# A two-block transformer on one core: cross attention fed tile by tile from an output scaled in PSUM, and the last feed-forward's weight sums made at four places

## The chip, the cores and the metric

The program runs on one core of one Trainium2 chip. The metric is the device time of one execution in microseconds (us), of which the median over three runs is given. The core has a matrix engine (TensorE, PE), a vector engine (VectorE, DVE), a scalar engine (ScalarE, ACT), a general engine (GpSimd, POOL), and SyncE (SP), which only issues transfers here. Each engine runs its own instructions in order, and they meet at semaphores. Transfers between HBM and the on-chip memory SBUF are made by 16 DMA engines, which all queues share; TensorE writes its products to PSUM, which VectorE and ScalarE read.

## The reference, cut to what matters

Two transformer blocks of width 1024 on 512 tokens (the second has 16 more). What the change touches:

```python
def first_block(...):
    h = h + hybrid_mixer(rmsnorm(h, norm_mix_g[l]), ...)           # ends with y_all @ w_out
    h = h + memory_cross_attention(rmsnorm(h, norm_xa_g[l]), mem, norm_mem_g[l],
                                   w_xq[l], w_xk[l], w_xv[l], w_xo[l])
    h = h + sqrelu_mlp(rmsnorm(h, norm_ff_g[l]), w_ff1[l], w_ff2[l])
    ...
def memory_cross_attention(hn, mem, ...):
    q = (hn @ w_q).reshape(b, s, XA_HEADS, XA_HEAD_DIM)            # 4 heads of 128
    logits = jnp.einsum("bshd,bmhd->bhsm", q, k) * (1.0 / math.sqrt(XA_HEAD_DIM))
    p = jax.nn.softmax(logits, axis=-1)
    ...
def gla_mixer(h, w_in, w_a1, w_a2, b_a, g_out, w_out):
    ...
    return (o * jax.nn.silu(r)) @ w_out                            # o normalised per head
def swiglu(h, w_in, w_out):
    gate, up = jnp.split(h @ w_in, 2, axis=-1)
    return (jax.nn.silu(gate) * up) @ w_out
```

## The kernel before, in words

**Products.** Activations lie feature-major: `h` holds 8 tiles of 128 features by 528 tokens. Every float32 operand is split into a high and a low part of a faster type, and a product is three matmuls (hi by hi, low by hi, hi by low). Weights come in units of 1 MB (128 x 2048): SP loads a unit to `w_raw` (two buffers), ScalarE writes `w_hi` (L491), VectorE, in some layers GpSimd, writes `w_lo = w_raw - w_hi` (L498), each two buffers deep. `sp_unit` loads unit u as soon as the low part of unit u-2 is made. A tile's sum lies in PSUM in `lin[slot]`, slot 0 or 1 with two banks each; whoever takes it out raises `lin_taken0` or `lin_taken1`, and TensorE waits for that before it reuses the slot (`deep=True` uses both banks of a slot, and waits for one tile less).

**Norms.** A layer's RMS norm is applied after its product: as each tile of `h` is finished, ScalarE writes the high part of the next operand (L794) and the tile's square (L912), VectorE the low part (L917, `dve_operand`), and GpSimd adds up the squares (L932, `pool_squares`). When all eight squares are added, TensorE sums over the partitions (L952, `pe_squares`), ScalarE takes the root, VectorE the reciprocal (L1001, `dve_root`), and the product is scaled by `scale_d`.

**From the mixer to cross attention.** `WB` is the second half of the mixer's output product (8 tiles, two units). `dve_mix_output` takes each tile out: it multiplies by `scale_d` into `tmp` (L737) and adds that to `h` (L740), then writes the low part of the tile before. `pe_cross` then makes the four query tiles (`query(t)`, L1807, 24 matmuls each, two tiles a unit), with the eight operand tiles waited for one by one in `query(0)`; between `query(0)` and `query(1)` stand the norm's sums. `logits(0)` (L1817) needs query 0 scaled (L1924), and so the reciprocal. The low parts of the next weight units are VectorE's: one in the middle of the mix output, one ahead of `dve_root`.

**Quads.** In the feed-forward layers most weight units are "quad" units: a product of 2 x 2 blocks is made with 7 block products in place of 8, and needs sums of weight blocks. These sums are made in HBM by transfers that GpSimd issues, in rounds for each group of layers ("ff1", "up0", "up1"): `pool_quad_base` copies the units to `weight_sums` (L385), `pool_quad_pairs` adds one block to another (L391, L393), `pool_quad_triples` (L399) and `pool_quad_fours` (L407) go on from there, each round after the one before has landed. The up1 group (parts a, b, c with 5, 7 and 5 units, for the last feed-forward, from 1667 us on) has its rounds issued from the queue of GpSimd between its other work, in program order. SP loads for a quad unit three blocks (L419), one sum (L421), and, when the last quad's `w_sum` buffer is free, the other three sums (L425, 768 KB).

**Gated linear attention (GLA).** `GR` is its gate product (8 tiles of 528 tokens, in 4 units); GpSimd makes the low parts of its weights (`dve_splits(pool, GR, nc.gpsimd)`). `dve_gates` takes each tile out (L1010), ScalarE applies silu (L2415), GpSimd multiplies it with the attention's output (`pool_gates`, L2464), VectorE scales it (L2487), ScalarE writes the high part (L2432) and VectorE the low part (L2492). The next product, `GOUT`, begins with `pe_first_pair` (L608): its two first tiles, with these eight operands waited for.

## Time and profile before

| | |
|---|---|
| median of 3 runs | 2020.7 us (2017.12 to 2021.94) |
| profiled execution, its own time | 2011.54 us |
| span of its trace | 2009.7 us |
| mean granted clock of TensorE | 0.991 of full speed |
| busy: PE, DVE, ACT, POOL | 97%, 63%, 42%, 15% of the span |

The profile is of one execution. Times in its views are microseconds from the start of the span; 1.8 us of the execution's time lie outside the span. "Busy" of the matrix engine includes pipelined matmuls whose ends are modelled, so its waits are read from single rows rather than from its share.

### The profile page before, as it was taken

How to read it: one execution, taken by the hardware profiler on the slowest of the kernel's cores; microseconds unless marked ns; L12 is line 12 of the kernel's file. 1: busy time of each engine (PE TensorE's matmuls, PEld its weight loads, DVE VectorE, ACT ScalarE, POOL GpSimd, SP SyncE). 2: the span in 40 equal slices, each digit the busy share in tenths (PEclk: the TensorE clock that was granted, in tenths of full speed). 3: DMA queues.
4: the chain of work that ended last, by engine and by line, in shares of the span. 5: the costliest groups of instructions: out<-in, count | busy, mean ns of one | idle time of the engine just before them, and what ended most of it. 6: DMA issues, size and time to landing. Idle time of an engine off the chain costs nothing.

```text
span 2009.7 us, 29776 instructions
## 1 busy us (share of the span) xinstructions
PE 1939.4 (97%) x12259; PEld 1709.5 (85%) x12259; DVE 1269.4 (63%) x1770; ACT 838.5 (42%) x1140; POOL 305.2 (15%) x249
## 2 busy tenths in 40 slices
PE   7999998999999899999999999999998899999998
PEld 6788866788898888999999999999885578889896
DVE  6668767666574664121658577476798658668475
ACT  4448744433142344223444143244534445234243
POOL 2122241200110141011420000002144110000002
PEclk9999999999999999998999999999998999999999
DMA  9854131499999758810165343343221023344251
GB/s 332 218 120 146 64 89 65 178 352 248 221 246 337 275 128 199 171 50 35 65 165 191 121 148 137 116 152 117 83 84 54 22 100 132 125 157 159 100 186 66
DMA packets 68480, 299.14 MB, mean 149 GB/s; under 512 B 6505, under 2 KB 6633, under 8 KB 48386
## 3 DMA queue, kind: packets, MB, share of 16 engines
q1 hardware_dynamic: 38064, 201.15, 27.9%
q0 software_dynamic: 30128, 96.08, 20.2%
q8 instruction: 95, 1.56, 0.3%
q14 instruction: 31, 0.25, 0.0%
q10 hardware_dynamic: 162, 0.10, 0.0%
HBM read 295.19 MB, written 94.96 MB: 194 GB/s over the span
## 4 chain that ended last, share of the span: by engine, by line
PE 55%; issue 27%; DVE 9%; ACT 3%; DMA 3%; POOL 2%; SPq 0%; POOLq 0%; DVEq 0%; ACTq 0%
PE lin L584 32%; PE lin L2015 7%; PE aux L2015 5%; DMA w_sum<-weight_sums 2%; DVE scores L2781 1%; DVE best L2776 1%; PE lin L1807 1%; PE aux L1605 1%; PE aux L2911 1%; POOL squares L932 1%; ACT w_hi L491 1%; DMA w_raw<-in_weights 1%; PE lin L1560 1%; DVE w_lo L498 1%; PE lin L2881 1%
## 5 line engine op out<-in xcount | busy, mean ns | idle before, releaser
L584 PE MATMUL lin<-x_hi,w_hi 128*128 128x512 f32 (+1 forms) x1128 | 397.2, 352 | 9.4 <-issue 2.9
L584 PE MATMUL lin<-x_hi,w_lo 128*128 128x512 f32 (+1 forms) x1128 | 396.0, 351 | 0.0
L584 PE MATMUL lin<-x_lo,w_hi 128*128 128x512 f32 (+1 forms) x1128 | 395.5, 351 | 0.0
L498 DVE TENSOR_TENSOR w_lo<-w_raw,w_hi 128x2048 fp32r<-128x2048 f32 (+1 forms) x102 | 231.0, 2265 | 144.7 <-ACT w_hi L491 144.3
L491 ACT ACTIVATE w_hi<-w_raw 128x2048 fp32r<-128x2048 f32 (+1 forms) x112 | 210.3, 1878 | 207.7 <-PE lin L584 193.1
L584 PEld LDWEIGHTS lin<-x_hi,w_hi 128*128 128x128 f32 x1128 | 211.9, 188 | 43.1 <-issue 6.7
L584 PE MATMUL lin<-v_hi,w_hi 128*128 128x264 f32 (+1 forms) x704 | 236.7, 336 | 6.1 <-DVE tmp L2567 3.5
L584 PEld LDWEIGHTS lin<-x_lo,w_hi 128*128 128x128 f32 x1128 | 212.0, 188 | 29.9 <-issue 0.2
L584 PEld LDWEIGHTS lin<-x_hi,w_lo 128*128 128x128 f32 x1128 | 212.0, 188 | 29.7
L584 PE MATMUL lin<-v_hi,w_lo 128*128 128x264 f32 (+1 forms) x704 | 233.5, 332 | 0.0
L584 PE MATMUL lin<-v_lo,w_hi 128*128 128x264 f32 (+1 forms) x704 | 233.1, 331 | 0.0
L932 POOL TENSOR_TENSOR squares<-squares,tmp 128x512 f32<-128x512 f32 (+2 forms) x64 | 87.3, 1364 | 617.8 <-ACT tmp L912 615.2
L584 PEld LDWEIGHTS lin<-v_hi,w_hi 128*128 128x128 f32 x704 | 133.9, 190 | 21.7 <-issue 7.8
L584 PEld LDWEIGHTS lin<-v_lo,w_hi 128*128 128x128 f32 x704 | 133.9, 190 | 13.3 <-issue 0.5
L584 PEld LDWEIGHTS lin<-v_hi,w_lo 128*128 128x128 f32 x704 | 133.8, 190 | 12.6
L456 DVE TENSOR_TENSOR w_lo<-w_raw,w_hi 128x512 fp32r<-128x512 f32 x129 | 110.4, 865 | 39.6 <-ACT w_hi L433 20.1
L433 ACT ACTIVATE w_hi<-w_raw 128x512 fp32r<-128x512 f32 x43 | 27.1, 631 | 196.5 <-PE lin L2015 109.2
L2015 PE MATMUL aux<-v_hi,w_hi 128*128 128x256 f32 (+1 forms) x344 | 97.0, 282 | 0.4 <-DVE tmp L2041 0.4
L2015 PE MATMUL aux<-v_hi,w_lo 128*128 128x256 f32 (+1 forms) x344 | 97.3, 283 | 0.0
L2015 PE MATMUL lin<-vt_lo,w_hi 128*128 128x256 f32 (+1 forms) x344 | 97.1, 282 | 0.0
L2015 PE MATMUL lin<-vt_hi,w_hi 128*128 128x256 f32 (+1 forms) x344 | 97.0, 282 | 0.0
L2015 PE MATMUL aux<-v_lo,w_hi 128*128 128x256 f32 (+1 forms) x344 | 96.8, 281 | 0.0
(481 smaller groups left out, 4437.1 us busy)
## 6 DMA issues: line engine op xcount, KB each, us to landing
w_raw<-in_weights SPq DMA_DIRECT2D x112, 1024.0 KB, 4.8
w_raw<-in_weights SPq DMA_DIRECT2D x43, 768.0 KB, 6.0
w_sum<-weight_sums SPq DMA_DIRECT2D x43, 768.0 KB, 4.7
weight_sums<-in_weights POOLq DMA_DIRECT2D x4, 5120.0 KB, 48.7
weight_sums<-in_weights POOLq DMA_DIRECT2D x2, 7168.0 KB, 56.2
w_raw<-weight_sums SPq DMA_DIRECT2D x43, 256.0 KB, 6.3
weight_sums<-in_weights POOLq DMA_DIRECT2D x8, 1280.0 KB, 13.9
weight_sums<-weight_sums POOLq DMA_DIRECT2D x8, 1280.0 KB, 12.5
```

The lines of the kernel that those rows point to most:

```text
L433: nc.scalar.activation(w_block(w_hi, unit, 1, 2), w_block(w_raw, unit, 1, 2), ACT.Copy)\
L456: nc.vector.tensor_tensor(w_block(w_lo, unit, a, b), w_block(w_raw, unit, a, b), w_block(w_hi, unit, a, b).bitcast(F32), ALU.subtract)\
L491: nc.scalar.activation(w_hi[:, s, 0:n], w_raw[:, s, 0:n], ACT.Copy).then_inc(sem("w_hi_ready"), 1)
L498: does.tensor_tensor(w_lo[:, s, 0:n], w_raw[:, s, 0:n], w_hi[:, s, 0:n].bitcast(F32), ALU.subtract).then_inc(sem("w_lo_ready"), 1)
L584: last = nc.tensor.matmul(o, a, b, start=(k % (L.kc // k_banks) == 0 and p == 0), stop=((k + 1) % (L.kc // k_banks) == 0 and p == 2))
L932: nc.gpsimd.tensor_tensor(acc, acc, tmp[:, s, 0:N.n], ALU.add).then_inc(sem("square_added"), 1)
L1560: mm = nc.tensor.matmul(lin[1][64 * (hd % 2):64 * (hd % 2) + 64, 1, P * j:S1], v_tok[:, j, 64 * hd:64 * hd + 64], w_att[:, SB_AT[j]:SB_AT[ ...
L1605: mm = nc.tensor.matmul(o, wp[:, k, t % 4 * P:t % 4 * P + P], xp_[:, k, 0:S1], start=(k == 0 and r == 0), stop=(k == 3 and r == 2))
L1807: mm = nc.tensor.matmul(lin[slot][:, 0, :], wp[:, k, m * P:m * P + P], xp_[:, k, 0:S1], start=(k == 0 and p == 0), stop=(k == KD - 1 and p ...
L2015: mm = nc.tensor.matmul(bank[:, b, 0:hf], wp, xp_, start=(k == 0 and p == 0), stop=(k == 3 and p == 2))
L2776: ins = nc.vector.max(best[:, n - 1, :], scores_of(n))
L2781: ins = nc.vector.match_replace(scores_of(n), best[:, n - 1, :], scores_of(n), TAKEN)
```

## The change

- **The mix output.** The product is scaled in place, in PSUM, and then added to `h` from there; `lin_taken` is raised by the add and `h_added` by a no-operation behind it. The split of the next weight unit stands two tiles earlier on ScalarE and on VectorE.
- **Cross attention.** The first two query tiles are made together (`first_queries`): operands 0 to 3 for the one and then the other, then operand after operand for both. The norm's sums come behind both, and then 14 matmuls whose product nobody reads. The low part of the second query unit moves from VectorE to GpSimd.
- **GLA's end.** `pe_first_pair` takes operands 0 to 3 for its first tile, 0 to 3 for its second, and 4 to 7 for both, one by one. The last gate tile is taken out and passed through silu after operand 3 and ahead of operands 4 to 7.
- **The up1 sums.** GpSimd issues the copies of part b where all three stood, those of a and c only behind the squares of the next norm, and the three transfers of the triples one by one between GR's four weight units.

```diff
@@ dve_mix_output
-                ht, out_t = h_tile(t, S1), tmp[:, 2 + t % 2, 0:S1]
+                ht, out_t = h_tile(t, S1), lin[slot][:, t // 2 % 2, 0:S1]
                 dve.wait_ge(sem("lin_done"), n + 1)
-                nc.vector.tensor_tensor(out_t, lin[slot][:, t // 2 % 2, 0:S1], scale_d[:, 0:S1], ALU.mult)\
-                    .then_inc(sem(f"lin_taken{slot}"), 1)
+                link(dve, nc.vector.tensor_tensor(out_t, out_t, scale_d[:, 0:S1], ALU.mult))
+                nc.vector.tensor_tensor(ht, ht, out_t, ALU.add).then_inc(sem(f"lin_taken{slot}"), 1)
                 dve.wait_ge(sem(f"lin_taken{slot}"), before + 1)
-                nc.vector.tensor_tensor(ht, ht, out_t, ALU.add).then_inc(sem("h_added"), 1)
-                dve.wait_ge(sem("h_added"), base + t + 1)
+                nc.vector.engine_nop().then_inc(sem("h_added"), 1)
                 if t:
                     dve_operand(dve, l_xa, t - 1)
-                if t == 5:
+                if t == 3:
                     next_lo(dve, WB, 1, 0)
@@ pe_cross (a step is the three matmuls of L1807)
+                pe.wait_ge(sem("w_lo_ready"), w_unit + 1)
+                for m in range(2):
+                    slot, before, _ = XQ.tile(0, m, 0)
+                    pe.wait_ge(sem(f"lin_taken{slot}"), before - 1)
+                    for k in range(4):
+                        if m == 0:
+                            l_xa.wait_operand(pe, k)
+                        step(m, k)
+                for k in range(4, KD):
+                    l_xa.wait_operand(pe, k)
+                    for m in range(2):
+                        mm = step(m, k)
+                        if k == KD - 1:
+                            mm.then_inc(sem("lin_done"), 1)
@@
-            query(0)
+            first_queries()
             pe_squares(pe, l_xa)
-            query(1)
+            for _ in range(14):
+                nc.tensor.matmul(lins[:, 1, 0:S1], v_hi[:, 0, 0:P], v_hi[:, 0, 0:S1], start=True, stop=True)
             logits(0)
@@ dve_cross
-            next_lo(dve, XQ, 0, 0)
             dve_root(dve, l_xa)
             taken(0)
             taken(1)
             maxima(0)
+            dve.wait_ge(sem("w_lo_ready"), XQ.unit0 + 2)
             next_lo(dve, XQ, 1, 0)
@@ pe_first_pair
-                for k in range(L.kc - 1):
+                for k in range(L.kc // 2):
                     if m == 0:
                         ready(k)
                     step(m, k)
-            ready(L.kc - 1)
-            for m in range(2):
-                step(m, L.kc - 1).then_inc(sem("lin_done"), 1)
+            for k in range(L.kc // 2, L.kc):
+                ready(k)
+                for m in range(2):
+                    mm = step(m, k)
...
@@ dve_gates, t == KD - 1
-                    for k in range(KD - 1):
+                    for k in range(4):
                         scaled(k)
                         if k:
                             lo(k - 1)
-                    lo(KD - 2)
...
-            scaled(KD - 1)
+            for k in range(4, KD):
+                scaled(k)
+                lo(k - 1)
             lo(KD - 1)
@@ the queue of GpSimd
             pool_squares(pool, l_xa, l_ssd.idx + 1)
+            next_lo(pool, XQ, 0, 0, nc.gpsimd)
             pool_squares(pool, l_ff, l_ff.idx)
...
-            pool_quad_base(pool, "up1", *"abc")
+            pool_quad_base(pool, "up1", "b")
             pool_squares(pool, l_mix0, l_mix0.idx)
+            pool_quad_base(pool, "up1", *"ac")
             pool_quad_pairs(pool, "up1")
-            pool_quad_triples(pool, "up1")
             next_splits_after(pool, GR)
-            dve_splits(pool, GR, nc.gpsimd)
+            for u in range(GR.units):
+                next_lo(pool, GR, u % 2, u // 2, nc.gpsimd)
+                if u < len(SUM_RUNS["up1"]):
+                    pool_quad_triple(pool, "up1", u)
             pool_gates(pool)
```

The order of instructions on VectorE in the mix output, its first tiles, before (L737 scales, L740 adds, L917 is the low part of the tile before):

```order
L737 TENSOR_TENSOR tmp<-lin,scale_d 128x512
L740 TENSOR_TENSOR h<-h,tmp 128x512
L917 SCALAR_TENSOR_TENSOR v_lo<-h,col,v_hi 128x512
L498 TENSOR_TENSOR w_lo<-w_raw,w_hi 128x2048
L737 TENSOR_TENSOR tmp<-lin,scale_d 128x512
L740 TENSOR_TENSOR h<-h,tmp 128x512
```

That piece is from tiles 5 and 6. The corresponding piece of the change, from tiles 3 and 4 (the lines have moved by 6 to 9):

```order
L746 TENSOR_TENSOR lin<-lin,scale_d 128x512
L747 TENSOR_TENSOR h<-h,lin 128x512
L749 ISA
L925 SCALAR_TENSOR_TENSOR v_lo<-h,col,v_hi 128x512
L504 TENSOR_TENSOR w_lo<-w_raw,w_hi 128x2048
L746 TENSOR_TENSOR lin<-lin,scale_d 128x512
L747 TENSOR_TENSOR h<-h,lin 128x512
```

The scaled product no longer passes through `tmp`, each tile has one no-operation more, and the weight's low part stands two tiles earlier. On TensorE the place behind the last operand now reads (L960 the norm's sum, L1889 the 14 idle matmuls, L1849 the first logits):

```order
L1812 MATMUL lin<-v_hi,w_hi 128x512
L1812 MATMUL lin<-v_lo,w_hi 128x512
L1812 MATMUL lin<-v_hi,w_lo 128x512
L960 MATMUL aux<-squares,cst 128x512
L1889 MATMUL lin<-v_hi 128x512 x14
L1849 MATMUL aux<-k_t,xq_t 128x256 x4
```

Before, the 24 matmuls of query 1 stood between the norm's sum and the logits; they now stand ahead of the sum. On GpSimd, between the copies of up1 and GLA's gates, before:

```order
L385 DMA weight_sums<-in_weights 128x5x2048
L385 DMA weight_sums<-in_weights 128x7x2048
L385 DMA weight_sums<-in_weights 128x5x2048
L925 MEMSET squares 128x1056
...
L399 DMA weight_sums<-weight_sums 128x5x512
L399 DMA weight_sums<-weight_sums 128x7x512
L399 DMA weight_sums<-weight_sums 128x5x512
...
L498 TENSOR_TENSOR w_lo<-w_raw,w_hi 128x2048
```

and with the change:

```order
L385 DMA weight_sums<-in_weights 128x7x2048
L933 MEMSET squares 128x1056
...
L385 DMA weight_sums<-in_weights 128x5x2048 x2
L391 DMA weight_sums<-in_weights 128x5x512
...
L504 TENSOR_TENSOR w_lo<-w_raw,w_hi 128x2048
L405 DMA weight_sums<-weight_sums 128x5x512
L504 TENSOR_TENSOR w_lo<-w_raw,w_hi 128x2048
L405 DMA weight_sums<-weight_sums 128x7x512
```

Two of the three copies move behind the eight rounds of squares (in a loop, whose rows are left out), and each triple stands behind a weight unit's low part.

## Rows read from the trace of the kernel before

**Rows 1.** The page: the span, and the chain that ended last.

```profile
span 2009.7 us, 29776 instructions
PE 55%; issue 27%; DVE 9%; ACT 3%; DMA 3%; POOL 2%; SPq 0%; POOLq 0%; DVEq 0%; ACTq 0%
```

**Rows 2.** Waits of PE: for whom, us in total, times, longest.

```profile
PE lin L1807 <- DVE w_lo L498: 6.3, 1, 6.3
...
PE lin L584 <- DVE h L689: 2.9, 2, 1.6
...
PE lin L608 <- DVE x_lo L2492: 1.0, 3, 0.4
```

**Rows 3.** Windows over ff1c's and ff1d's quads: stretch, length, PE busy (matmuls), others.

```profile
564.43:594.23 29.80, 29.80 (x254) 29.80 (x253) 24.08 (x34) 13.28 (x19) 3.17 (x2) 1.00 1.05 244
650.00:686.18 36.18, 30.27 (x252) 29.75 (x252) 23.89 (x34) 13.21 (x18) 0.00 (x0) 1.00 0.96 356
```

**Rows 4.** The three-sums load: the page's median, then 622 to 645 us.

```profile
w_sum<-weight_sums SPq DMA_DIRECT2D x43, 768.0 KB, 4.7
w_sum<-weight_sums SPq DMA_DIRECT2D x1, 768.0 KB, 20.4
```

**Rows 5.** Timeline of POOL: start, us, instruction, idle before it.

```profile
449.46 1.47 POOL L391 DMA_DIRECT2D weight_sums<-in_weights  x1 [66.01 <-DMA weight_sums<-in_weights]
...
602.81 2.42 POOL L385 DMA_DIRECT2D weight_sums<-in_weights  x2
...
736.70 1.48 POOL L391 DMA_DIRECT2D weight_sums<-in_weights  x1
...
798.04 1.44 POOL L393 DMA_DIRECT2D weight_sums<-in_weights  x1 [10.88 <-issue]
...
871.84 4.55 POOL L498 TENSOR_TENSOR w_lo<-w_raw,w_hi 128x2048 fp32r<-128x2048 f32 x1 [36.66 <-ACT w_hi L491]
```

**Rows 6.** Plain weight loads (L416), all 110: from issue to landing.

```profile
DMA to landing us min/median/max: 4.6/4.8/17.1
```

**Rows 7.** Timelines of SP and ACT: one load and the split that needs it.

```profile
738.93 0.33 SPq L416 DMA_DIRECT2D w_raw<-in_weights  x1
...
760.22 1.92 ACT L491 ACTIVATE w_hi<-w_raw 128x2048 fp32r<-128x2048 f32 x1 [11.35 <-PE lin L584]
```

**Rows 8.** Timelines of DVE and POOL in the mix output.

```profile
297.11 0.68 DVE L737 TENSOR_TENSOR tmp<-lin,scale_d 128x512 f32<-128x512 f32 x1
297.83 1.78 DVE L740 TENSOR_TENSOR h<-h,tmp 128x512 f32<-128x512 f32 x1
299.65 0.75 DVE L917 SCALAR_TENSOR_TENSOR v_lo<-h,col,v_hi 128x512 fp32r<-128x512 f32 x1
...
297.76 1.30 POOL L932 TENSOR_TENSOR squares<-squares,tmp 128x512 f32<-128x512 f32 x1 [1.91 <-ACT tmp L912]
```

**Rows 9.** Timelines of DVE and POOL where the add reads PSUM.

```profile
360.17 0.68 DVE L689 TENSOR_TENSOR h<-h,lin 128x512 f32<-128x512 f32 x1
...
360.07 1.34 POOL L932 TENSOR_TENSOR squares<-squares,tmp 128x512 f32<-128x512 f32 x1 [44.87 <-ACT tmp L912]
```

**Rows 10.** The chain in cross attention: start, us, what.

```profile
306.47 7.21 PE lin L1807 x24
313.68 0.86 PE aux L952 x2
314.53 5.59 PE lin L1807 x24
```

**Rows 11.** Timelines of DVE and ACT around the norm's root.

```profile
305.69 0.68 DVE L737 TENSOR_TENSOR tmp<-lin,scale_d 128x512 f32<-128x512 f32 x1
...
315.96 3.35 DVE L1001 RECIPROCAL scale_d<-scale_d 128x512 f32<-128x512 f32 x1
...
314.57 0.69 ACT L982 ACTIVATE scale_d<-aux,eps_t 128x512 f32<-128x512 f32 x1 [0.86 <-PE aux L952]
```

**Rows 12.** A window behind the long wait; third from the end is the granted clock.

```profile
306.40:309.20 2.80, 2.73 (x7) 2.18 (x8) 2.73 (x4) 1.24 (x2) 0.90 (x2) 0.50 0.82 281
```

More of the change, by code:

```diff
@@ L400, in pool_quad_triples, with pool_quad_triple @@
                     .then_inc(sem("sum_s2"), 16)
+        def pool_quad_triple(pool, group, n):
+            pool.wait_ge(sem("sum_pair"), 2 * sums_made(group))
+            run = SUM_RUNS[group][n]
+            pool.dma_start(quad_rows(run, w_sums, 1, 2), quad_rows(run, w_sums, 3, 4), accum_op=ALU.add)\
+                .then_inc(sem("sum_s2"), 16)
         def pool_quad_fours(pool, group):
@@ L619, in pe_first_pair @@
                     step(m, k)
-            ready(L.kc - 1)
-            for m in range(2):
-                step(m, L.kc - 1).then_inc(sem("lin_done"), 1)
+            for k in range(L.kc // 2, L.kc):
+                ready(k)
+                for m in range(2):
+                    mm = step(m, k)
+                    if k == L.kc - 1:
+                        mm.then_inc(sem("lin_done"), 1)
         def act_evacuate(act, L, tile, after=None):
@@ L724, in act_mix_output @@
                 act_operand(act, l_xa, t, t % 2)
-                if t == 4:
+                if t == 2:
                     next_hi(act, WB, 1, 0)
@@ L1795, in pe_cross, with first_queries, step @@
             w_unit = XQ.unit0
+            def first_queries():
+                w = [x[:, w_unit % 2, :].rearrange("p (k n) -> p k n", k=KD) for x in (w_hi, w_lo)]
+                def step(m, k):
+                    slot = XQ.tile(0, m, 0)[0]
+                    for p, (wp, xp_) in enumerate(((w[0], v_hi), (w[0], v_lo), (w[1], v_hi))):
+                        mm = nc.tensor.matmul(lin[slot][:, 0, :], wp[:, k, m * P:m * P + P], xp_[:, k, 0:S1],
+                                              start=(k == 0 and p == 0), stop=(k == KD - 1 and p == 2))
+                    return mm
+                pe.wait_ge(sem("w_lo_ready"), w_unit + 1)
[11 more added lines that the diff above has]
+                        if k == KD - 1:
+                            mm.then_inc(sem("lin_done"), 1)
             def query(t):
@@ L2448, in act_gates @@
                             scale(e)
+                    silu(t)
+                    if t == 7:
                         for k in range(4, 7):
                             hi(k)
-                    silu(t)
                     if t == 5:
```

2 lines of the change are left out of this document (removed).

## The prediction

> **What bounds the kernel now.** I read the page first: the chain that ended last is TensorE's for more than half the span, and another quarter is "issue", time with nothing shown to wait for, much of it stretches in which TensorE runs and the chain was followed along another engine's queue [rows 1]. So time is won where TensorE stands still. The view of waits, for TensorE, gives the places: 6.3 us in one piece ahead of cross attention's first query, and in GLA's last product three short waits for operands and one for `h` [rows 2] (the 2.9 us are two waits; the one in GLA, 1.6 us, is the longest). One loss is not named there as a wait for data; two windows show it. ff1c's three quads take 29.8 us with 254 matmuls. ff1d's, the same work, take 36.2 us, with TensorE busy for 30.3 [rows 3]. The view of transfers says why: the load of the three block sums, 4.7 us in the median, took 20.4 us there [rows 4], and the timeline of GpSimd shows what it shared the DMA engines with, the copies of up1, issued from 602.81 us on [rows 5].
>
> **Part 1, the sums of up1.** The up1 copies are 17 units. up0's, of the same size, kept GpSimd waiting 66.0 us until 449.46 us [rows 5]. With the change only b's 7 units are copied behind 602.8 us: 66 x 7/17 = 27 us, more while weight loads run beside them, so they land between 630 and 640 us. The first quad of ff1d needs its sums at about 641 us, the two others later, by when nothing runs beside their loads. I take the whole difference of the two windows, 36.2 - 29.8 = **-6.4 us** [rows 3]. Bounds: nothing, if b alone fills the stretch; 6.4, since ff1c is the same work with no wait.
>
> The copies of a and c move behind 736.7 us. Ten units at the same rate are 39 us, with loads beside them up to 51, so the pairs begin at some 788 us at the latest instead of 736.70. Their issue took from 736.70 to 799.5 us [rows 5], 63 us, so GpSimd is through at about 851 us; it next has to be there at 871.84 us, for the low part of GR's weights, which ScalarE releases [rows 5]: 21 us to spare, **cost nothing**. Queued behind those transfers on GpSimd are GR's four low parts, whose readers are TensorE and SP's next load, and then GLA's gates. The triples are issued behind a low part each, 1.5 us, in time that GpSimd idles: nothing, too. The plain loads meet the copies instead. A load issued at 738.93 us is needed by the split at 760.22, which waited for TensorE and not for it [rows 7]: 21.3 us to spare, and the slowest of all 110 plain loads, those beside the copies of now among them, took 17.1 [rows 6]. Nothing again, with a small reserve.
>
> The Trainium skill (DMA: Bandwidth & Descriptors, "Issuing engines are not separate DMA queues") says that transfers issued from any engine run on the same 16 DMA engines and interleave. That speaks against this part: the copies are as large at 736 us as at 602. By it alone the 6.4 us would be paid elsewhere and the sum would be -5.0; the rows above say that the loads there have room which ff1d's have not. What hangs on it is the first rival.
>
> **Part 2, the mix output and cross attention.** The add of SBUF to SBUF took 1.78 us beside GpSimd's squares, whose instruction ran 1.30 us, and it ended half a microsecond behind it. The low part took 0.75, the scaling out of PSUM 0.68 [rows 8]. An add with the product in PSUM took 0.68 us inside a GpSimd instruction of the same kind [rows 9]. So with the change the add falls to 0.68, though the low part, which still reads two SBUF operands, will sometimes meet GpSimd and lose some tenths. A tile took 0.68 + 1.78 + 0.75 = 3.2 us, and takes 0.68 + 0.68 + 0.75 and about 0.2 for the no-operation and such a meeting, 2.3 to 2.4. Tile 4 began at 297.11 [rows 8]; it loses about one microsecond of earlier holds and gains the 2.3 us weight split that now stands ahead of it: 298.5. Four tiles more at 2.4 bring the last operand at about 308.5.
>
> TensorE's wait of 6.3 us is put down to the weight split, but it ended at 306.47, 0.1 us behind the scaling of tile 6 (305.69 + 0.68) [rows 10, 11]: it was the slot. That is now needed for tile 4 only, whose add ends at 299.9, before TensorE is done with the product ahead at 306.47 - 6.3 = 300.2. It begins there, with operands 0 to 3, and has 24 matmuls of two tiles before it needs operand 4. At 0.233 us (5.59 / 24 [rows 10]) the 48 matmuls end at 311.4; operand 7 is wanted at about 310, so 308.5 is early enough, and the squares are added by 310. There is no slow clock either: seven matmuls behind the 6.3 us wait ran at a granted clock of 0.50, the lower of the two levels, 1.2 GHz [rows 12], 0.4 us each, some 1.2 us lost.
>
> From the norm's sum it goes on in series: 0.86 (sum), 0.69 (root), 3.35 (reciprocal), 0.69 (query 0 scaled) and 0.3 between them, 5.9 us [rows 10, 11]. Before, the reciprocal began 0.7 us behind the root's end, VectorE being at a weight split; that split is now GpSimd's (4.55 us for one of this size [rows 5]), from 310.1 to 314.8, wanted at about 319 for query 2. The logits begin at 311.4 + 5.9 = 317.3 instead of 314.53 + 5.59 = 320.1: **-2.8 us**, less than the 6.3, because query 1 no longer covers the root. The 14 idle matmuls take 3.3 of these 5.9 us and cost nothing. What follows the logits keeps its distance. Bounds: -0.5, if VectorE is held as before (then only the reciprocal's 0.7 us goes), and -4, if the clock and the operands leave no seam.
>
> The Trainium skill (SBUF — State Buffer, "Who interferes with whom") has it that a VectorE instruction with two SBUF inputs, and not one with a single one, contends with a GpSimd instruction that reads SBUF. The adds agree (1.78 against 0.68), no row of before shows a long reciprocal beside GpSimd. By the rule it stays at 3.35; were it held until 314.8, the term would be -1.2.
>
> **Part 3, GLA's end.** The last gate tile's silu, gate and scaling stood behind seven operands, and the last operand, the weight split and the first addition to `h` behind them. With the tile taken out after operand 3, its own silu, gate and scaling run beside operands 4 to 6. I put the last operand about 2 us earlier (an estimate: some three instructions of 0.7 us, as those of [rows 8], leave the series), and ScalarE and VectorE come to the next split and the first `h` by as much. TensorE's waits there, 1.0 us for operands and 1.6 for `h` [rows 2], shrink to about 0.5: **-2.1 us**. Bounds 0 and -2.6.
>
> **The sum.** -6.4 - 2.8 - 2.1 = -11.3 us against the profiled execution's 2011.54: 2000.2. The median of the runs is 9.2 us above that execution, so the same difference from it gives **2009.4 us**. No change and this measurement differ by up to 0.3%, 6 us.
>
> **Rivals.**
> - *The copies are paid for in GLA.* If loads beside them take over 21.3 us, each split waits. For: transfers were at the limit in ff1d [rows 4]. Against: 17.1 at most [rows 6]. At 23 us for three units the price is about 5: 2014.5. Chance 0.13.
> - *b alone still disturbs ff1d.* It is the largest part; if it lands at 655 us, one of the loads is still slow and half of the 6.4 stays: 2012.6. Chance 0.12.
> - *Cross attention gives nothing.* The low parts take the adds' place in being held, or the last operand comes late: -0.5 in place of -2.8, 2011.7. Against: only one of three VectorE instructions a tile is left that can be held. Chance 0.1.
> - *Slower: GpSimd comes late to GR.* Copies and pairs in series must be issued by 871.84 us; from there each microsecond later costs one. It decides past 871.84 + 11.3 = 883 us, when the 114 us of both take 28% longer than I reckon; at 895 the kernel takes 2033. Chance 0.05.
>
> **How the numbers follow.** All three parts as reckoned, 0.6, own range 2006 to 2013, 2009.4 at its middle. The second and third rival lie inside or at its edge, the first within 0.3%. Range 2004 to 2016: below, the bounds of parts 2 and 3 (-1.7) and the spread of the medians before; above, the first rival. Faster by over 0.3% (below 2014.6) holds for the likeliest case, the second and third rivals and a part of the first: 0.82. Within 0.3%: 0.12. Slower: 0.06.
>
> **What the changed profile would show.** ff1d's quads at about 30 us and the three-sums loads near 5 us in the last two quads; the adds at 0.69 us, no wait of TensorE ahead of cross attention, the logits 5.9 us behind the norm's sum; GpSimd idle ahead of GR's first low part, released by ScalarE; no split in 740 to 860 us released by a DMA; no wait for `h` at GLA's end above 0.6 us. A weight load above 21 us, or GR's low part released by a transfer, would make the prediction wrong.

## The result, and the profile after

Five runs of the changed kernel took 2002.86 us in the median (2000.47 to 2009.09), five of before beside them 2019.62 (2017.12 to 2021.94): ratio 0.9922, 95% interval 0.9903 to 0.9941. The kernel is faster, and by more than forecast: 2009.4 was predicted, with a range from 2004 to 2016. The profiled execution took 2002.86 us. Against the profiled execution of before (2011.54) that is -8.7 us, against the medians -16.8; half of this study is about that disagreement. A median of five runs carries scatter of its own: 13 runs of the changed kernel, taken together further down, have a mean of 2004.6 us, inside the forecast range.

The page of the changed kernel, its span and its chain; TensorE has a larger share of the chain:

```profile
span 2001.0 us, 29796 instructions
PE 62%; issue 23%; DVE 8%; ACT 3%; POOL 3%; DMA 1%; SPq 0%; POOLq 0%; DVEq 0%; ACTq 0%
```

Windows over ff1c's and ff1d's quads, as [rows 3] (stretch, length, then busy time of PE, PEld, DVE, ACT and POOL with instructions, granted clock, DMA share, GB/s):

```profile
561.42:591.22 29.80, 29.80 (x253) 29.76 (x253) 24.20 (x35) 13.34 (x19) 3.17 (x2) 1.00 1.03 240
646.88:676.44 29.56, 29.56 (x252) 29.56 (x251) 24.09 (x34) 13.11 (x18) 0.00 (x0) 1.00 0.37 134
```

ff1d's quads took 29.6 us in place of 36.2, and the DMA engines were busy for 0.37 of the stretch in place of 0.96. Of ff1d's three three-sums loads the first (issued at 618.77 us) still took 20.2 us, ahead of the first quad and harmless; the others took 4.6 and 4.4. The copy of b, issued at 599.36 us, took 40.7 us where 27 and "more" were reckoned; it was there at 640 us, 7 us before the first quad.

GpSimd's timeline, as [rows 5]:

```profile
726.96 1.75 POOL L385 DMA_DIRECT2D weight_sums<-in_weights  x2
767.97 1.47 POOL L391 DMA_DIRECT2D weight_sums<-in_weights  x1 [39.26 <-DMA weight_sums<-in_weights]
...
825.08 1.44 POOL L393 DMA_DIRECT2D weight_sums<-in_weights  x1 [9.41 <-issue]
865.33 4.56 POOL L504 TENSOR_TENSOR w_lo<-w_raw,w_hi 128x2048 fp32r<-128x2048 f32 x1 [38.80 <-ACT w_hi L497]
```

The copies of a and c were there after 41 us (39 to 51 were reckoned), the last pair was issued at 825, and GpSimd then stood still for 38.8 us until ScalarE released GR's low part. The plain loads issued beside the copies (727 to 870 us) took 4.7 to 11.5 us; nothing waited for one.

The chain in cross attention, as [rows 10]:

```profile
300.14 11.18 PE lin L1812 x48
311.32 0.87 PE aux L960 x2
312.19 0.02 issue
312.21 0.70 ACT scale_d L990
312.91 0.02 issue
312.94 3.36 DVE scale_d L1009
316.30 0.02 issue
316.32 0.70 DVE xq_t L1957
317.02 0.04 issue
317.07 1.99 PE aux L1849 x8
```

The logits begin at 317.07 where 317.3 was forecast, 3.05 us before those of the kernel before. The reciprocal took 3.36 us though GpSimd's weight split ran beside it until 314.2, so the prediction's -1.2 for that case did not come. VectorE and GpSimd in the mix output, as [rows 8]: the adds take 0.69 us, and where something is held it is the low part, which still reads two SBUF operands:

```profile
301.11 0.69 DVE L747 TENSOR_TENSOR h<-h,lin 128x512 f32<-128x512 f32 x1
301.83 1.10 DVE L925 SCALAR_TENSOR_TENSOR v_lo<-h,col,v_hi 128x512 fp32r<-128x512 f32 x1
...
301.08 1.30 POOL L940 TENSOR_TENSOR squares<-squares,tmp 128x512 f32<-128x512 f32 x1 [1.59 <-ACT tmp L920]
```

The end of GLA. First two windows of before: its last product, and what TensorE then waits for the first addition to `h`; then the same two of the changed kernel.

```profile
970.25:983.50 13.25, 12.27 (x97) 11.63 (x95) 8.45 (x12) 6.71 (x11) 1.79 (x2) 1.00 0.00 0
983.50:985.37 1.87, 0.28 (x3) 0.10 (x2) 1.73 (x2) 0.05 (x1) 0.00 (x0) 1.00 0.00 0
```

```profile
965.18:976.78 11.60, 11.60 (x97) 11.48 (x95) 10.27 (x12) 5.85 (x9) 2.20 (x2) 1.00 0.00 1
976.78:977.24 0.46, 0.28 (x4) 0.10 (x2) 0.31 (x1) 0.06 (x1) 0.00 (x0) 1.00 0.00 0
```

15.1 us became 12.1. So the three places together gained 3.05 + 6.6 + 3.05 = 12.7 us, yet the end came only 8.7 sooner. Windows over the whole stretch between ff1d's quads and GLA's last product, of before and of the changed kernel, show where the rest went:

```profile
686.18:970.25 284.07, 281.86 (x1962) 258.19 (x1963) 105.59 (x128) 98.98 (x137) 66.12 (x36) 0.98 0.46 114
676.44:965.18 288.74, 286.53 (x1964) 262.84 (x1962) 105.00 (x127) 99.81 (x139) 67.17 (x38) 0.96 0.56 148
```

The same work took 4.7 us longer at a lower granted clock: TensorE spent 13.7 us of it at the low level (0.50) in the one execution and 23.9 in the other, which at half speed is 5.1 us lost. Nothing but GpSimd's own transfers waited for a DMA there, though the copies of a and c now run beside this work. Kernels below speak against them as the cause, with one execution each: from the norm's sum ahead of GLA to the next layer's, e_sums, with the copies there, took 290.90 us at a clock of 0.96, and m_psum, without them, 291.01 at 0.97, c_before 294.10 at 0.96.

Of the waits of TensorE in the changed kernel one is new:

```profile
PE lin L2916 <- ACT v_all L2842: 5.2, 1, 5.2
```

It lies in the attention stage, which the change does not touch; before, this wait was 1.1 us. VectorE's timeline there, first of before, then of the changed kernel, then GpSimd's of the changed kernel:

```profile
1476.39 3.44 DVE L1088 RECIPROCAL rstd<-rstd 128x528 f32<-128x528 f32 x1
1479.87 1.45 DVE L1097 SCALAR_TENSOR_TENSOR c_t<-c_t,col,rstd 128x528 f32<-128x528 f32 x2
```

```profile
1468.36 3.44 DVE L1096 RECIPROCAL rstd<-rstd 128x528 f32<-128x528 f32 x1
1471.83 5.90 DVE L1105 SCALAR_TENSOR_TENSOR c_t<-c_t,col,rstd 128x528 f32<-128x528 f32 x2
```

```profile
1472.53 4.63 POOL L504 TENSOR_TENSOR w_lo<-w_raw,w_hi 128x2048 fp32r<-128x2048 f32 x1 [6.57 <-ACT w_hi L497]
```

The two scalings of `c_t` read two SBUF operands each. In before GpSimd's weight split began at 1480.58, with the second scaling already begun, and was itself held (5.24 us for 4.63). In the changed kernel the second scaling was held through the whole split: the pair took 5.90 us against 1.45. VectorE's top-k, the longest work of the stage, stands behind it. The Trainium skill (SBUF — State Buffer, "Who interferes with whom") says that a VectorE instruction's second SBUF input comes through a port that it shares with GpSimd, and that the shared pair is "an exclusive lock". The rows agree that the one held waits for the other's instruction to end. They don't tell who gets the lock: VectorE's recorded start was 0.03 us ahead of GpSimd's in before, where it was spared, and 0.01 us ahead in the changed kernel, where it was held.

Yet this is not where the 4.0 us are missing. The attention stage from TensorE's last product ahead of it to its own last product, of before, of the changed kernel, and of a kernel tested below (f_after), where `c_t` is spared on purpose:

```profile
1516.60:1597.04 80.44, 65.87 (x267) 38.59 (x268) 60.61 (x135) 40.40 (x108) 29.18 (x35) 0.92 0.07 21
1508.55:1588.40 79.85, 62.50 (x267) 37.81 (x268) 64.12 (x148) 41.41 (x112) 29.15 (x35) 0.94 0.07 21
1508.99:1584.29 75.30, 61.07 (x268) 36.59 (x268) 60.48 (x135) 40.40 (x108) 29.18 (x35) 0.98 0.08 22
```

With `c_t` held the stage took 0.6 us less than before with it spared. The changed kernel lost 4.1 us at the start of the stage; before lost 4.7 us more than it further on. Part of that is low clock, 13.6 us at the low level against 10.2, which is worth 1.7 us at most; where the rest went is not shown. So in this pair the shortfall is the clock in the GLA stretch, and not `c_t`, though sparing `c_t` can pay, as f_after shows.

### The profile page after: what moved, and what is told of

It is laid out like the page before. It is cut to its first block, busy times and chain, and to the rows that moved or that the text cites. A ratio compares the mean times of both kernels' runs of the same rounds, so it can differ in the third digit from the quotient of the medians.

```text
span 2001.0 us, 29796 instructions
## 1 busy us (share of the span) xinstructions
PE 1940.7 (97%) x12273; PEld 1714.6 (86%) x12273; DVE 1267.6 (63%) x1769; ACT 838.4 (42%) x1140; POOL 309.1 (15%) x250
## 3 DMA queue, kind: packets, MB, share of 16 engines
q0 software_dynamic: 30128, 96.08, 20.2%
## 4 chain that ended last, share of the span: by engine, by line
PE 62%; issue 23%; DVE 8%; ACT 3%; POOL 3%; DMA 1%; SPq 0%; POOLq 0%; DVEq 0%; ACTq 0%
PE lin L590 36%; PE lin L2048 7%; PE aux L2048 5%; DVE scores L2816 1%; DVE best L2811 1%; PE aux L1613 1%; POOL squares L940 1%; PE aux L2946 1%; PE lin L1568 1%; PE lin L2916 1%; PE aux L2384 1%; ACT w_hi L497 1%; PE aux L2398 1%; DVE scores L2794 1%; DMA w_raw<-in_weights 1%
## 5 line engine op out<-in xcount | busy, mean ns | idle before, releaser
L590 PEld LDWEIGHTS lin<-x_hi,w_lo 128*128 128x128 f32 x1128 | 212.0, 188 | 29.6
L590 PEld LDWEIGHTS lin<-v_lo,w_hi 128*128 128x128 f32 x704 | 134.9, 192 | 13.3 <-issue 0.5
L462 DVE TENSOR_TENSOR w_lo<-w_raw,w_hi 128x512 fp32r<-128x512 f32 x129 | 110.4, 866 | 38.8 <-ACT w_hi L439 20.1
## 6 DMA issues: line engine op xcount, KB each, us to landing
weight_sums<-in_weights POOLq DMA_DIRECT2D x8, 1280.0 KB, 13.3
```

Of the source, the lines that this page charges most:

```text
L462: nc.vector.tensor_tensor(w_block(w_lo, unit, a, b), w_block(w_raw, unit, a, b), w_block(w_hi, unit, a, b).bitcast(F32), ALU.subtract)\
L590: last = nc.tensor.matmul(o, a, b, start=(k % (L.kc // k_banks) == 0 and p == 0), stop=((k + 1) % (L.kc // k_banks) == 0 and p == 2))
```

## The experiments

Each kernel was timed in a series of 5 to 12 runs. The table is what each gave; a ratio is to the runs of before on the same chip (17 to 35 of them, medians 2018.6, 2020.4, 2021.0 and 2019.6 us for the four chips), and the mean clock is the mean over the runs of TensorE's granted clock as a share of full speed. The five runs of each kernel shown with the result are not in it.

| kernel | runs | median us | mean clock | ratio to before (95%) |
|---|---|---|---|---|
| before, four chips | 100 | 2018.6 to 2021.0 | 0.986 to 0.987 | |
| c_before | 12 | 2015.7 | 0.988 | 0.9992 (0.9977 to 1.0007) |
| e_sums | 12 | 2009.3 | 0.989 | 0.9963 (0.9950 to 0.9975) |
| e_cross | 12 | 2015.6 | 0.988 | 0.9986 (0.9971 to 1.0000) |
| e_gla | 12 | 2013.9 | 0.987 | 0.9983 (0.9968 to 0.9998) |
| c_after | 8 | 2003.0 | 0.990 | 0.9934 (0.9910 to 0.9958) |
| f_after | 6 | 2000.0 | 0.990 | 0.9920 (0.9892 to 0.9947) |
| i_after | 12 | 2009.5 | 0.992 | 0.9951 (0.9934 to 0.9968) |
| n_idle | 12 | 2007.5 | 0.988 | 0.9934 (0.9913 to 0.9955) |
| m_psum | 12 | 2017.0 | 0.988 | 0.9974 (0.9958 to 0.9990) |
| q_early | 12 | 2021.0 | 0.988 | 1.0003 (0.9989 to 1.0017) |
| l_abc | 6 | 2004.9 | 0.990 | 0.9910 (0.9889 to 0.9931) |
| i2_after | 5 | 1999.1 | 0.992 | 0.9894 (0.9876 to 0.9911) |
| w_idle | 12 | 2019.7 | 0.989 | 1.0000 (0.9982 to 1.0019) |
| no_q | 6 | 2004.8 | 0.988 | 0.9940 (0.9917 to 0.9963) |
| best | 6 | 1998.1 | 0.992 | 0.9901 (0.9880 to 0.9923) |

**c_before**: no edit.

> The kernel before, unchanged, as a control: what spread do its runs have, and why did its profiled execution (2011.5 us) lie 8 us under its timed runs (2017 to 2022)? Theory A, a coin toss in the attention stage: the second scaling of c_t on VectorE (two SBUF inputs) starts within 0.1 us of GpSimd's weight split; where GpSimd wins it is held for 4.5 us, and the profiled execution of before had won. Then a profile of another execution with the loss shows 5.9 us for the pair in place of 1.45, and runs come in two groups some 4 us apart at the same clock. Theory B, the granted clock: runs differ by the mean clock alone, 0.99 in the fast and 0.98 to 0.985 in the slow, and the time falls on a line with it. Theory C, the up1 copies slow ff1d by an amount that differs from execution to execution: the window of ff1d's quads shows 36 us here and over 40 elsewhere, at the same clock. Ratio to the other runs of before: 1.000.

Theory B holds for the spread: 12 runs from 2010.9 us at a mean clock of 0.992 to 2024.4 at 0.984, in between on a line. What a run loses to the low level is (1 - mean clock) x its time; over all kernels one us more of that goes with 0.76 us more time. As the low level is 0.50, that is 0.38 us for each us spent at it, less than the half that TensorE itself loses. What is left scatters by 1.7 us. By that line the profiled execution of before, at 0.9906 where the mean of before is 0.9866, belongs at 2012.8 us; it took 2011.5. So the clock accounts for 6.2 of the 7.4 us that it lay under the mean of before (2018.9), and the rest is within the scatter.

Theory C falls: the window of ff1d's quads is 36.1 us again. Of theory A the toss is real, but it does not show at the end. The `c_t` pair of this execution of the same kernel reads

```profile
1484.60 5.90 DVE L1097 SCALAR_TENSOR_TENSOR c_t<-c_t,col,rstd 128x528 f32<-128x528 f32 x2
```

Of the 13 kernels profiled with this place unchanged, the first profile of before is the only one that was spared. In the other twelve the recorded starts of the split and of the second scaling lie within 0.03 us of each other too, and VectorE is held. But this execution, which ended 4.0 us after the first, was 4.7 us behind it already at the last product ahead of the attention stage (1521.33 us against 1516.60), and the stage took 79.74 us with `c_t` held against 80.44 with it spared. The execution against which the prediction made its sum stood apart by its clock, in GLA above all: 13.7 us at the low level from 676 to 970 us, where the other twelve have 20.5 to 37.0, but for no_q with 13.7.

**e_sums, e_cross, e_gla**: one part of the change each, on the kernel before. The sums:

```diff
-            pool_quad_base(pool, "up1", *"abc")
+            pool_quad_base(pool, "up1", "b")
             pool_squares(pool, l_mix0, l_mix0.idx)
+            pool_quad_base(pool, "up1", *"ac")
             pool_quad_pairs(pool, "up1")
-            pool_quad_triples(pool, "up1")
             next_splits_after(pool, GR)
-            dve_splits(pool, GR, nc.gpsimd)
+            for u in range(GR.units):
+                next_lo(pool, GR, u % 2, u // 2, nc.gpsimd)
+                if u < len(SUM_RUNS["up1"]):
+                    pool_quad_triple(pool, "up1", u)
```

> Before, with only the sums of up1 spread (b early, a and c behind the squares, triples between GR's low parts). By the prediction's sum: -6.4 us, ff1d's quads at about 30 us, and nothing paid later, 0.9968. Rival, the sums are worth more in the timed runs than in the profiled pair, since the copies' harm to ff1d's loads differs between executions: -9 to -12 us, 0.9945 or lower. Rival, GLA pays part of it back: -3 us, with splits in 740 to 860 us released by a DMA.

0.9963 is -7.5 us (-10.1 to -5.0). The quads of ff1d took 29.7 us, no split in GLA waited for a load. The prediction's -6.4 lies inside the interval; no payback is seen.

The cross part is the edit of the diff in `dve_mix_output`, `pe_cross`, `dve_cross` and GpSimd's one line.

> Before, with only the mix output scaled in PSUM, cross attention's first queries begun early, the 14 idle matmuls and GpSimd's split of XQ's first unit. By the prediction's sum: -2.8 us (0.9986), logits 5.9 us behind the norm's sum. The comparison of the two profiles says -3.0. Rival, that something of the cross part makes the rest of the measured -16.8 us, for instance less time at the low clock later on: -5 us or more. In the profiled execution the attention stage may add 4.5 us or not, as GpSimd or VectorE wins at c_t.

0.9986 is -2.8 us (-5.9 to 0); the logits began at 317.28 here. The `c_t` scaling was held, as the last sentence allowed.

The end of GLA is the edit in `pe_first_pair` and in the two loops around the last gate tile.

> Before, with only the end of GLA changed (the last gate tile taken out after operand 3, the last product's second half by operands). By the prediction's sum: -2.1 us (0.9990). The comparison of the two profiles says -3.1 for the stretch 970 to 985 us, of which about 1 may be a low clock at another place. Rival: it moves the c_t scaling of the attention stage against GpSimd's split and so wins or loses 4.5 us there: a result of +1 to +2 or of -6 us.

0.9983 is -3.4 us (-6.5 to -0.4). The two windows of GLA's end, here of e_gla, are those of the changed kernel to a tenth:

```profile
974.83:986.40 11.57, 11.57 (x96) 11.45 (x95) 10.25 (x12) 5.90 (x10) 2.02 (x2) 1.00 0.00 0
986.40:986.90 0.50, 0.33 (x4) 0.14 (x2) 0.33 (x1) 0.08 (x1) 0.00 (x0) 1.00 0.00 0
```

The three add to -13.7 us.

**c_after**: the changed kernel again.

> The changed kernel, unchanged, for a longer series. The three parts alone gave -5.5, -1.0 and -3.0 us at equal granted clock, and two of them a mean clock higher by 0.0019 and 0.0015, worth 2.7 and 2.3 us at 0.72 us for each us of low clock. If the parts simply add, the series stands 14.5 us under before (0.9928), 9.5 of it at equal clock. Rival: the five runs of the result (-16.8 us in the medians) are right and the parts help each other: 0.9917. Rival: the prediction's -11.3 us was right and five runs too few: 0.9944.

0.9934, -13.3 us (-18.2 to -8.5), which fits that the parts add, though the interval is too wide to show it. This holds the prediction's ratio too (0.9944), so this series alone would not have refuted it; by the means of all 13 runs of the changed kernel (2004.6) and the 112 of before in the table (2018.9) the gain is 14.3 us. Some 5 us of it go with a higher clock (0.990 against 0.987): by the line of c_before the kernels differ by 9.4 us at equal clock, near the 8.7 of the two profiled executions, which stand at 0.991 both.

**f_after**: GpSimd's last low part of AQ waits for `c_t`.

```diff
-            dve_splits(pool, AQ, nc.gpsimd)
+            for u in range(AQ.units):
+                if u == AQ.units - 1:
+                    n_kv.wait(pool, "ready", 2)
+                next_lo(pool, AQ, u % 2, u // 2, nc.gpsimd)
```

> The changed kernel, and GpSimd's last low part of AQ waits until both tiles of c_t are scaled, so that VectorE's second scaling of c_t (two SBUF inputs) is never held beside a 4.6 us split. Where the pair took 5.9 us in the changed kernel it takes 1.45, the top-k ends 4.45 us sooner and TensorE's wait for v_all (5.2 us) shrinks to about 1. If all of that reaches the end: -4 us, 0.998 of the changed kernel, 0.9907 of before. Rival: the waits behind it grow in place of it (in the profiled execution of before, which was spared, 4.6 us ahead were followed by 3.5 and 1.7 us less lead), so it gives -1 us or nothing.

VectorE's and GpSimd's timelines of f_after:

```profile
1472.27 1.45 DVE L1105 SCALAR_TENSOR_TENSOR c_t<-c_t,col,rstd 128x528 f32<-128x528 f32 x2
...
1473.79 4.65 POOL L504 TENSOR_TENSOR w_lo<-w_raw,w_hi 128x2048 fp32r<-128x2048 f32 x1 [7.39 <-DVE c_t L1105]
```

TensorE's wait for `v_all` fell from 5.2 to 1.1 us and the profiled end came 4.3 us sooner, with the stage at 75.3 us in place of 79.9; the median is 3.0 lower than c_after's, though the intervals overlap. The edit that lets GpSimd wait 0.8 us saves VectorE 4.45.

**i_after** and **i2_after**: f_after with idle matmuls in TensorE's waits behind it (11 and 6, then 3 and 1).

```diff
+            def idle(n):
+                for _ in range(n):
+                    nc.tensor.matmul(aux[:, 0, 0:S1], aq_t[:, 0, 0:P], k_all[:, 0, 0:S1], start=True, stop=True)
```

> As the kernel with the c_t scaling spared, and 11 idle matmuls ahead of the third turn of head 0 and 6 ahead of the second turn of head 1, where TensorE waited 3.4 and 2.1 us. If it is TensorE's standing still that brings the low clock at 1510 to 1536 us (6.8 to 14 us of it in all profiles so far), the stretch runs at full clock and gains 2 to 5 us over the kernel without them. Rival: the low clock there comes from the many short matmuls and not from the waits, or falls elsewhere instead: 0, and +0.5 us from idle matmuls that end too late.

> The kernel with the c_t scaling spared and idle matmuls in the attention stage again, at their true length. With 11 and 6 the low clock at 1510 to 1536 us was gone, but in this type one is executed as two of 0.43 us, so that they ended 6 and 3 us after the operands were there. Now 3 and 1, 2.6 and 0.9 us in waits of 3.4 and 1.1 us. If the idle matmuls keep the clock and delay nothing: 1 to 3 us under the kernel that only spares the c_t scaling, 1998 us in the median, and no low clock at 1510 to 1525. Rival: so few don't hold the clock, or it falls somewhere else instead: the same as without them, 2000 to 2001.

Windows over the same 14 us, of the changed kernel, of f_after and of i2_after; the third number from the end is the granted clock:

```profile
1508.00:1522.00 14.00, 6.36 (x22) 3.85 (x21) 12.77 (x35) 5.39 (x16) 5.19 (x7) 0.71 0.12 39
```

```profile
1508.00:1522.00 14.00, 8.74 (x38) 5.64 (x37) 12.49 (x28) 6.81 (x18) 9.00 (x11) 0.88 0.12 39
```

```profile
1508.00:1522.00 14.00, 10.95 (x46) 5.84 (x44) 13.30 (x32) 7.27 (x19) 9.00 (x11) 1.00 0.12 39
```

The granted clock is 0.71 with the wait of 5.2 us, 0.88 without it, 1.00 with idle matmuls. Only the last of these steps is firm: c_after, the changed kernel again, has 0.83 in this window with the same wait of 5.2 us. In the first 40 us of the stage the three kernels with idle matmuls here (i_after, i2_after, best) have no low clock at all, the other fourteen 3.4 to 17.0 us of it. But in those three it comes later, 3.4 to 6.8 us from 1575 us on, where f_after and the changed kernel have none; over the whole stage i2_after has 3.4 us, as f_after has, and took 75.8 us against 75.3. So the rival that the low clock falls elsewhere instead came true.

i_after was 9.5 us slower than f_after in the median: its 11 idle matmuls ran for 9.6 us where 2.6 were meant, since one between `f32` operands took 0.87 us and one between `fp32r` operands takes 0.23. In i2_after they ended before the operands came. It took 1999.1 us, 0.9 less than f_after, which 5 runs can't tell from nothing.

**n_idle**: the changed kernel without the 14 idle matmuls ahead of the logits.

> The changed kernel without the 14 idle matmuls in front of the logits; TensorE then stands still for some 4.5 us from the norm's sum to the logits. The prediction booked them as free and nothing more. If a still TensorE brings the low clock, a low stretch appears behind 313 us, as it did at 303 in before: +2 to +4 us, mean clock lower by 0.0015. Rival: the clock stays up and the time is the same, +0.

TensorE, without them, executed the logits and the next query at half clock, here a window of n_idle:

```profile
316.00:322.00 6.00, 4.99 (x12) 3.98 (x13) 2.69 (x5) 0.07 (x1) 0.00 (x0) 0.50 0.36 150
```

and what follows came 2.6 us later. The ratio is that of c_after; its mean is 2.4 us above that of the changed kernel's 13 runs, with an uncertainty of about 4: seen in the trace, not settled by the times.

**m_psum** and **q_early**: each half of the cross part alone on the kernel before. The first is the edit of `dve_mix_output` with the two splits moved, the second the rest.

> Before, with only the mix output changed: the product stays in PSUM, the add reads it there, the next layer's splits stand after tiles 2 and 3. Which half of the cross part gives the gain? If the mix output alone does it: tile 6 is out at some 304.5 us in place of 306.4, TensorE stands still 4.3 us in place of 6.3, the weight split that holds the reciprocal comes 3 us sooner, and the logits begin at 317.3 as in the whole part: -2.8 us. Rival, both halves are needed: the queries in series behind a slot leave the logits at 319 to 320, -0.5 to -1, and the low clock at 303 stays, since TensorE still stands still. The whole part measured -3.3 in the means (-1.0 at equal clock, the rest by a higher clock).

> Before, with only the other half of the cross part: first queries begun by operands, 14 idle matmuls, GpSimd's split of XQ's first unit; the adds of the mix output still read two SBUF operands. The last operand then comes at about 311.4 us as in before, the two last steps, the norm's sum and the 5.9 us in series behind it put the logits at 318.9: -1.2 us, plus 2 us less low clock if TensorE's early start keeps it up; -1.2 to -3. Rival: the adds are held even longer beside GpSimd's squares and the 4.6 us split, and it gives nothing, 0.

m_psum gave 0.9974, -5.2 us (-8.5 to -2.0); its logits began at 318.37, 1.8 us sooner than in before, and the query behind them 2.0 us ahead, where the whole part gives 3.0. The interval ends just short of the trace's 1.8; at equal clock the times say -0.8 (uncertainty 1.0). q_early gave nothing in the times (+0.6 us, -2.2 to +3.4). In its trace the logits began at 324.53, 4.4 us later than before and 5.6 later than expected, a miss; at equal clock its times are 4.5 us longer. Its chain:

```profile
303.70 2.21 DVE w_lo L498
305.92 0.04 issue
305.96 12.82 PE lin L1804 x48
318.78 0.87 PE aux L952 x2
319.67 0.70 ACT scale_d L982
320.39 3.36 DVE scale_d L1001
323.78 0.70 DVE xq_t L1949
324.48 0.04 issue
324.53 1.99 PE aux L1841 x8
```

I had forgotten that both first queries need the low part of their weights, which VectorE makes behind tile 5 at 303.70 to 305.92. TensorE began at 305.96, half a microsecond sooner than before (306.47), but with both queries ahead of the norm's sum in place of one, and nothing beside the root and the reciprocal.

**l_abc**: the changed kernel with b's copies moved as well.

```diff
-            pool_quad_base(pool, "up1", "b")
             pool_squares(pool, l_mix0, l_mix0.idx)
-            pool_quad_base(pool, "up1", *"ac")
+            pool_quad_base(pool, "up1", *"abc")
```

> The changed kernel with b's copies moved behind the squares of the mix layer as well, all 17 units there. If b alone disturbs nothing in ff1d (its quads took 29.8 us in the changed kernel) and GLA's loads have room for more: 0, the copies landed by 795 us and the pairs issued by 858, before GpSimd is wanted at 865.3. Rival, what is moved into GLA costs there: low parts late from 865 on, +2 to +10 us, and splits released by a DMA. Rival, b still costs ff1d a little beside its plain units: -1 us.

The windows of ff1d's quads are the same (29.6 us), the 17 units took 66.9 us from 726.55, the last pair was issued at 857.79 and GR's first low part still waited for ScalarE, 5.6 us. 0.9910 and a mean 1.0 us lower: no difference that can be told. So b costs ff1d's quads nothing, and GLA has room for all of it, with 5.6 us left.

**w_idle**: before, with 24 idle matmuls in the 6.3 us wait.

```diff
+            l_xa.wait_operand(pe, 0)
+            for _ in range(24):
+                nc.tensor.matmul(aux[:, 3, 0:S1], v_hi[:, 0, 0:P], v_hi[:, 0, 0:S1], start=True, stop=True)
             query(0)
```

> Before, and 24 idle matmuls in the 6.3 us for which TensorE waited ahead of cross attention's first query; nothing comes sooner by them, they only keep TensorE running. If the part of the gain that goes with a higher mean clock comes from TensorE no longer standing still there: the 3.4 to 6.8 us of low clock at 303 to 311 us go, the 24 query matmuls run at 0.233 us from the first on, and the logits begin 1 to 1.5 us sooner; -1 to -2.5 us in the means, 0.999. Rival: the low clock there is not of this wait, or what it gives is swallowed by the reciprocal, which waits for VectorE's split and not for TensorE: 0.

A window of w_idle, to be laid beside [rows 12]:

```profile
306.40:309.20 2.80, 2.68 (x12) 2.20 (x13) 2.69 (x5) 1.25 (x2) 0.89 (x2) 1.00 0.89 275
```

Full clock and 12 matmuls in place of 7, and not a microsecond won: the norm's sum began at 313.45 (313.68 before), now behind GpSimd's last squares, and the reciprocal at 316.01 (315.96), behind VectorE's weight split. The 1.2 us that the prediction booked for the clock at this place were no loss of their own.

**no_q**: the changed kernel without the queries' half.

> The changed kernel without its half of the first queries (no early start, no 14 idle matmuls, VectorE splits XQ's first unit again), but with the mix output scaled in PSUM. Alone, the mix output gave -2.9 us in the means and the queries' half +2.2, so the two do not add. If the mix output carries the part: as the changed kernel within 1 us, 2004 to 2006 in the mean, with the low clock at 305 back. Rival: the queries' half is what keeps the clock up and is worth its 0.4 us in the profile and 1 to 2 us more: 2006 to 2007.

0.9940, the mean 1.0 us over that of the changed kernel, with an uncertainty of about 4. The trace is sharper: the logits began at 317.75, 0.7 us later than in the changed kernel. With the adds out of the way and the split early, the queries' half is worth about that.

**best**: the three edits of f_after, i2_after and l_abc together.

> The changed kernel with the c_t scaling spared, 3 and 1 idle matmuls in the attention stage and all of up1's copies behind the squares of the mix layer. The first two gave -4.6 us in the means against the changed kernel, the last -0.9, with an interval that holds 0. If they add: 1999 us in the mean, 0.990 of before. Rival, the last gives nothing: 2000.

1998.1 us, 0.9901. The three kernels with `c_t` spared and no late idle matmuls have 17 runs with a mean of 2000.2, the changed kernel 13 with 2004.6: 4.4 us, more than the uncertainty of the two means together (about 3). That sparing `c_t` is what does it rests on the traces (the stage took 75.3 to 77.4 us in these three and 78.5 us or more in all others); f_after's own mean is 2001.5, and what the other two edits add isn't resolved.

## Why the prediction was wrong

The direction and the places held, and of the mechanisms all but two; the number did not, by 6.5 us to the median and 1.1 us beyond the range.

*The sums of up1* (-6.4 forecast): the windows give -6.6, the times -7.5 (-10.1 to -5.0). The steps are there: the copies of a and c landed after 41 us, no plain load was late, GR's low part was released by ScalarE, no stall was left in ff1d. One was mis-sized without harm: b's copy took 40.7 us where 27 were reckoned, and was in time by 7. (By the rule quoted in that part the sum would have been -4.9, not -5.0.)

*The cross part* (-2.8): -3.05 in the trace, -2.8 in the times. Right in the sum, wrong in two of its parts, and so right in part by luck. The clock's 1.2 us were no term (w_idle), and the early queries, for which most of the working was done, give about 0.7 us of it; the adds in PSUM and the earlier split give the rest (m_psum, no_q).

*GLA's end* (-2.1, bounds 0 to -2.6): -3.05 in the trace and -3.4 in the times, outside its bounds. This term was mis-sized. The step that failed is "TensorE's waits there, 1.0 us for operands and 1.6 for `h`": the view of waits counted three pieces. The window over the product shows 13.25 us for work that takes 11.6, so 1.65 us were lost to operands, and 1.87 in front of the next product, 3.5 in all. The bound was read from a view that leaves out the small gaps.

*"The median of the runs is 9.2 us above that execution, so the same difference from it gives 2009.4"*, and with it the range. This is the step that weighs most. The 9.2 us were noticed and not explained. They are no property of the kernel: the execution had less low clock than most (6.2 us by the line of c_before), and the median of three, 2020.7, stands 1.8 us over the mean of 112 runs, 2018.9. That it was also spared at `c_t` does not show at its end. The miss of 6.5 us is then made up of four pieces: 1.8 us of that median; 1.4 us of terms, 12.7 us measured in the traces against 11.3; 1.7 us by which the five runs of the result (2002.86) lie below the mean of 13 (2004.6); and the 1.6 us between 2018.9 - 12.7 = 2006.2 and that mean, less than its uncertainty (about 2.4). Two of the four are scatter of few runs, and runs of before go from 2006 to 2030 us over all chips. The range allowed 1.7 us downward in bounds, and nearly nothing for that scatter: its low end of 2004 should have been some 2000.

Of the rivals none is seen. Copies paid in GLA: no split waited, and the 4.7 us that the stretch took longer go with the clock, for which e_sums against m_psum speaks. b disturbing ff1d's quads: l_abc excludes it. Cross giving nothing: excluded by the traces; the times alone (0 to -5.9) would not do it. GpSimd late to GR: 38.8 us early, and 5.6 with all copies moved.

Two things stay open. The changed kernel's mean clock was higher (0.990 against 0.987) and some 5 us of its 14.3 go with that; why it was higher is not shown, and w_idle shows that fewer low stretches may be worth nothing. So the agreement of 12.7 us with the longer series may be in part chance: at equal clock the kernels differ by 9.4. And what the idle matmuls are worth in time is not known.

## What to carry to other kernels

Before a sum is taken off a median, ask why the profiled execution stands apart from its runs, and take a second profile of the same kernel. Lay the two side by side stage by stage, each stage's length with its granted clock: a wait that one has and the other lacks is not yet the reason why they end apart, for a later stretch may pay it back. What a stage loses is read from a window over it against the same work undisturbed, not from the list of waits. An early start only helps where all that it needs is early, and a higher clock is worth something only where TensorE sets the end.

## What the runs showed of the hardware

Two instructions at a shared resource, with recorded starts within 0.03 us of each other in 13 executions, cost VectorE 4.45 us in twelve of them and GpSimd 0.6 us in one, and the recorded order does not tell which: VectorE stood 0.03 us ahead when it was spared (1480.55 and 1480.58 us) and 0.01 us ahead when it was held (1472.52 and 1472.53). The mean granted clock of one and the same kernel went from 0.983 to 0.991 in 35 runs on one chip, and the time from 2024.2 to 2013.4 with it; over all kernels a us at the low clock goes with 0.38 us more time, less than the half that the clock itself takes. Idle matmuls in a wait cleared the stretch behind it of low clock (1.00 in place of 0.88) and 3.4 us of it stood 60 us further on instead. A matmul of 128x512 between `f32` operands took 0.87 us, between `fp32r` operands 0.23.
